# The recurrent half, retention's inputs, retention and the last projection of the second block's first layer as one stage, with heads in pairs and rotations by whole groups

## The reference, cut to what matters

```python
def hybrid_ab(h, w_in, conv_w, conv_b, ga_w, ga_b, gx_w, gx_b, lam, w_out):
    proj = h @ w_in
    y, xr, q, k, v, g = split(proj, six parts of 512 columns)
    xr = causal_depthwise_conv(xr, conv_w, conv_b)              # 4 taps
    lru_out = rg_lru(xr, ga_w, ga_b, gx_w, gx_b, lam) * gelu(y)
    ret_out = retention(q, k, v) * silu(g)                      # 8 heads of 64
    return concatenate([lru_out, ret_out], -1) @ w_out          # h = h + this

def rg_lru(x, ...):
    r, i = sigmoid(block_diag(x, ga_w) + ga_b), sigmoid(block_diag(x, gx_w) + gx_b)
    log_a = -8 * r * softplus(-lam)
    a, u = exp(log_a), sqrt(-expm1(2 * log_a)) * (i * x)
    return scan over tokens of  h = a * h + u

def retention(q, k, v):       # computed by the kernel over all 512 tokens at once
    q, k = rotary(q), rotary(k) / 8
    s = (q @ k.T) * decay     # decay[i, j] = g_head ** (i - j) for j <= i, else 0
    o = s @ v
    return (o - mean(o)) * rsqrt(var(o) + eps)                  # over each head's 64
```

## Time and profile before

| | us |
|---|---|
| median of 3 timed runs | 3396.03 |
| lowest and highest | 3384.46, 3397.12 |
| the profiled execution, its own time | 3386.9 |
| its span, first to last instruction | 3385.1 |
| TensorE busy | 2859.4 |
| VectorE busy | 1150.0 |
| ScalarE busy | 751.9 |
| POOL busy | 124.9 |

### The profile page before, as it was taken

One profiled execution on the slowest core, in us unless ns is written; L12 is line 12 of the kernel. 1 busy time (PEld: TensorE's weight loads), 2 busy tenths in 40 slices (PEclk: granted clock), 3 DMA queues, 4 the chain that ended last, 5 costly groups with the idle time before them and its releaser, 6 DMA issues.

```text
span 3385.1 us, 32012 instructions
## 1 busy us (share of the span) xinstructions
PE 2859.4 (84%) x13512; PEld 1848.2 (55%) x13512; DVE 1150.0 (34%) x1622; ACT 751.9 (22%) x1114; POOL 124.9 (4%) x116
## 2 busy tenths in 40 slices
PE   6877799888759879888845597899979999979997
PEld 4534453333348443323333473688869875558886
DVE  3434421111243431111145413332332368433233
ACT  2233300100122210100034110321221255232121
POOL 1200200000000200000010000000000000000000
PEclk8988889999979979999977798899987979989999
DMA  7852269999812069999911100223223200022230
GB/s 266 300 175 63 114 282 428 428 428 427 364 39 86 31 279 428 428 428 427 423 68 52 50 25 25 99 88 112 81 84 78 50 26 1 1 100 87 87 105 39
DMA packets 122255, 601.00 MB, mean 178 GB/s; under 512 B 7184, under 2 KB 12560, under 8 KB 96256
## 3 DMA queue, kind: packets, MB, share of 16 engines
q1 hardware_dynamic: 117056, 584.27, 43.7%
q0 software_dynamic: 5056, 14.69, 1.4%
HBM read 596.84 MB, written 2.10 MB: 177 GB/s over the span
## 4 chain that ended last, share of the span: by engine, by line
PE 65%; DMA 15%; DVE 12%; ACT 5%; issue 1%; POOL 0%; DVEq 0%; ACTq 0%; POOLq 0%
PE psum L281 63%; DVE scratch L231 5%; ACT scratch L269 5%; DMA weight_ring<-in_w_exp_down 5%; DMA weight_ring<-in_w_exp_up 4%; DMA scratch<-in_w_exp_down 3%; DMA weight_ring<-in_w_exp_gate 2%; PE psum L296 2%; DVE scratch L2906 1%; DVE scratch L244 1%; DVE scratch L264 1%; DVE scratch L237 1%; DVE scratch L1288 1%; DMA weight_ring<-in_w_mod 1%; ACT L269 0%
## 5 line engine op out<-in xcount | busy, mean ns | idle before, releaser
L281 PE MATMUL psum<-scratch,scratch 128*128 128x512 f32 (+13 forms) x9424 | 1943.0, 411 | 186.3 <-DVE scratch L231 110.0
L281 PEld LDWEIGHTS psum<-scratch,scratch 128*128 128x128 f32 (+4 forms) x9424 | 1418.9, 189 | 699.0 <-issue 338.9
L281 PE MATMUL psum<-weight_ring,scratch 128*64 128x512 f32 (+2 forms) x2752 | 710.5, 618 | 103.6 <-ACT scratch L269 36.0
L281 PEld LDWEIGHTS psum<-weight_ring,scratch 128*64 128x64 f32 (+2 forms) x2752 | 242.2, 146 | 526.8 <-issue 398.7
L231 DVE TENSOR_TENSOR scratch<-weight_ring,scratch 128x2048 fp32r<-128x2048 f32 (+2 forms) x110 | 241.9, 2199 | 596.6 <-ACT scratch L269 590.2
L269 ACT ACTIVATE scratch<-psum 128x512 f32<-128x512 f32 (+5 forms) x322 | 185.3, 575 | 889.3 <-PE psum L281 565.6
L269 ACT ACTIVATE scratch<-weight_ring 128x2048 fp32r<-128x2048 f32 (+2 forms) x110 | 202.9, 1844 | 660.7 <-PE psum L281 624.6
L296 PE MATMUL psum<-consts,scratch 128*128 128x128 f32 (+1 forms) x984 | 165.2, 315 | 181.4 <-DVE scratch L237 84.0
L296 PEld LDWEIGHTS psum<-consts,scratch 128*128 128x128 f32 (+1 forms) x984 | 129.7, 169 | 232.5 <-issue 95.7
L231 DVE TENSOR_TENSOR scratch<-scratch,psum 128x512 f32<-128x512 f32 x92 | 63.3, 688 | 563.0 <-PE psum L281 561.5
L231 DVE TENSOR_TENSOR scratch<-scratch,scratch 128x512 fp32r<-128x512 f32 (+10 forms) x346 | 211.9, 612 | 83.1 <-ACT scratch L269 72.5
(11 more groups left out here) (100 smaller groups left out, 619.2 us busy)
## 6 DMA issues: line engine op xcount, KB each, us to landing
weight_ring<-in_w_exp_gate SPq DMA_DIRECT2D x40, 2048.0 KB, 18.8
weight_ring<-in_w_exp_up SPq DMA_DIRECT2D x38, 2048.0 KB, 20.6
weight_ring<-in_w_exp_down SPq DMA_DIRECT2D x38, 2048.0 KB, 20.7
weight_ring<-in_ffn_w SPq DMA_DIRECT2D x28, 2048.0 KB, 7.8
scratch<-in_w_exp_up SPq DMA_DIRECT2D x26, 2048.0 KB, 20.6
scratch<-in_w_exp_down SPq DMA_DIRECT2D x26, 2048.0 KB, 18.1
weight_ring<-in_w_mod SPq DMA_DIRECT2D x24, 2048.0 KB, 8.8
scratch<-in_w_exp_gate SPq DMA_DIRECT2D x24, 2048.0 KB, 20.6
```

The source lines that it names most:

```text
L281: ins = T.eng.matmul(out, lhsT, rhs, start=start, stop=stop)
```

## The change

The stages `Recurrent`, `RetentionInputs`, `Retention` and `ResidualOut` become the one stage `Recurrent` (KEY `"ab_out"`); the fences between them are gone and every engine's order is written anew. The buffers are laid out so that the whole stage fits: `u` and later the rotated k, v, the gate and the scores share places of x and of the recurrence.

- POOL's small loads wait for the stage before the norm and no longer for the norm.
- The units come in the order x, y, q, k, v, g, two each. ScalarE and VectorE go through phases; phase n first splits unit n + 2 and then does what stands under it: convolution in 0 and 1, gelu in 2 and 3, sigmoids in 3 and 4, exp and tanh for all four groups in 4, roots in 5, scans in 6, rotations of q in 5 and of k in 7, the copies of the turned q, of v, of the turned k and the silu in 8 to 11.
- The gates on TensorE stand before and after the first q unit; the turns of q stand between the two v units, those of k between the two g units.
- The copies of the turned q into `qT` wait also until k is rotated, since the rotations' two temporaries lie in the places of `qT` and `kT`.
- One rotation is five VectorE operations over all four token tiles and all eight heads (one of 2048 elements a partition, four of 1024); k's factor is in the copy of the turned bank.
- Two heads of a pair are multiplied from the two halves of 64 partitions, without padding; decay, centring, squares and scaling run once for a pair, the product with the gate is on POOL.
- The last projection is in two halves: chunks 0 to 3 of `catT` (recurrence) are multiplied and added to `h` as fills between the pairs of heads, chunks 4 to 7 afterwards.

The diff, cut to its core (removed lines only where they show a difference):

```diff
 class Recurrent(Nothing):
-    KEY = "lru"
+    KEY = "ab_out"
+    LOW, HIGH = (0, 4), (4, 8)
+    FILL, O, TURNED = (0, 2), (2, 3), (3, 4)
...
     def sync(self, Y):
+        for u in self.units.values():
+            u.load(Y)
+        self.k.ring.load(Y, "decay", self.k.dram["decay"])
+        project_out_sync(self.k, Y, self.KEY, self.k.dram["ab_w_out_2"])
     def pool(self, G):
         self.norm.pool(G)
-        k.fence(G, self.norm.key)
+        k.fence(G, self.before)
         k.loads(G, "lru", [...])
+        k.loads(G, "ret", [(self.cos, d["ret_cos"]), (self.sin, d["ret_sin"])])
+        for p in range(4):
+            self.gated(G, p)
...
+    def unit_pe(self, T, name, i):
+        hi, lo = u.ready(T, i)
+        banks = k.psum.of(("ret", name)) if i else k.psum.take(T, ("ret", name), self.HIGH if name in "qv" else self.LOW, 4)
+        ...
+    def scores_pe(self, T, p, kt):
+        run = k.psum.take(T, ("ret s", p, kt), self.HIGH, 2)
+        ...
+        for i in range(2):
+            q = slice(64 * i, 64 * i + 64)
+            mm(T, run[:, i, 0:n], self.kT[q, p, kt * P:(kt + 1) * P], self.qT[q, p, kt * P:S], True, True, ...)
+    def values_pe(self, T, p):
+        T.wait_ge(*k.at("free", "ret s", p, NT - 1))
+        ...
     def pe(self, T):
         self.norm.pe(T)
         k.fence(T, self.norm.key)
+        for i in range(2):
+            self.features_pe(T, "x", i)
+        for i in range(2):
+            self.features_pe(T, "y", i)
+        for j in (0, 1):
+            self.gates_pe(T, j)
+        self.unit_pe(T, "q", 0)
+        for j in (2, 3):
+            self.gates_pe(T, j)
+        self.unit_pe(T, "q", 1)
+        for i in range(2):
+            self.unit_pe(T, "k", i)
+        self.unit_pe(T, "v", 0)
+        self.turned_pe(T, "q", self.rot_q, self.LOW)
+        self.unit_pe(T, "v", 1)
+        self.unit_pe(T, "g", 0)
+        self.turned_pe(T, "k", self.rot_k, self.HIGH)
+        self.unit_pe(T, "g", 1)
+        for p in range(4):
+            for kt in (0, 1):
+                self.scores_pe(T, p, kt)
+            if p:
+                self.values_pe(T, p - 1)
+            self.fill_pe(T, p if p == 0 else p + 1)
+            for kt in (2, 3):
+                self.scores_pe(T, p, kt)
+            if p == 0:
+                self.fill_pe(T, 1)
+            if p >= 2:
+                self.out_turn_pe(T, p - 2)
+        self.fill_pe(T, 5)
+        self.values_pe(T, 3)
+        self.fill_pe(T, 6)
+        self.out_turn_pe(T, 2)
+        self.fill_pe(T, 7)
+        self.out_turn_pe(T, 3)
+        ...
+        for t in range(NT):
+            for half in range(2):
+                self.project_pe(T, 1, t, half)
...
     def act(self, A):
+        for phase in range(-2, 12):
+            if phase + 2 < 12:
+                u, i = self.plan[phase + 2]
+                u.hi(A, i)
+            ...
+            if phase == 4:
+                A.wait_ge(*k.at("lru rate"))
+                for j in range(4):
+                    act(A, self.a[:, j, :], self.r[:, j, :], ACT.Exp, scale=self.small[3][:, j:j + 1])
+                for j in range(4):
+                    act(A, self.r[:, j, :], self.r[:, j, :], ACT.Tanh, ("lru tanh", j), scale=self.small[2][:, j:j + 1])
+            ...
+            if phase == 8:
+                self.turned_act(A, "q", self.qT, 1.0)
+        ...
+        for p in range(4):
+            A.wait_ge(*k.at("ret centred", p))
+            ...
+            act(A, self.sq[...], self.o[:, :, p * P:(p + 1) * P], ACT.Square, ("ret squared", p))
+            A.wait_ge(*k.at("ret mean square", p))
+            act(A, self.var[:, p, :], self.var[:, p, :], ACT.Sqrt, ("ret root", p))
+            if p >= 1:
+                self.out_act(A, p - 1)
...
     def dve(self, V):
-        fill(V, self.xr, 0.0)
-        V.wait_ge(*k.at("loaded", "lru"))
+        fill(V, self.xr[:, :, 0:4], 0.0, ("xr zero",))
+        ...
+        for p in range(4):
+            self.decayed(V, p, 0)
+            if p:
+                self.centred(V, p - 1)
+            self.decayed(V, p, 2)
+            if p == 0:
+                self.fill_dve(V, 0)
+                self.fill_dve(V, 1)
+            else:
+                self.fill_dve(V, p + 1)
+                self.scaled(V, p - 1)
+        self.fill_dve(V, 5)
+        self.centred(V, 3)
+        self.fill_dve(V, 6)
+        self.scaled(V, 3)
+        self.fill_dve(V, 7)
+        ...
+    def rotated(self, V, name, out):
+        ...
+        tt(V, a.rearrange("p (t h d) -> p t h d", t=NT, d=32), x.rearrange("p t (h d) -> p t h d", d=32),
+           cos.to_broadcast([P, NT, 16, 32]), ALU.mult)
+        ...
+        for i in range(2):
+            tt(V, bs[:, :, :, i, :], xs[:, :, :, 1 - i, :], sin, ALU.mult, *names)
+        for i, op in enumerate((ALU.subtract, ALU.add)):
+            tt(V, os[:, :, :, i, :], as_[:, :, :, i, :], bs[:, :, :, i, :], op, ...)
-class RetentionInputs(Nothing):
-    ...
-class Retention(Nothing):
-    ...
 def plan(k, out):
-    first = Recurrent(k, "scatter1")
-    inputs = RetentionInputs(k, first)
-    stages += [first, inputs, Retention(k, first, inputs), ResidualOut(k, "ab_out", Retention.KEY, d["ab_w_out_2"], first.catT)]
+    stages.append(Recurrent(k, "scatter1"))
```

More of the change, by code:

```diff
@@ new lines, in out_turn_pe, with project_pe @@
+    def out_turn_pe(self, T, p):
+        k = self.k
+        T.wait_ge(*k.at("ret gated", p))
+        bank = k.psum.take(T, ("ret turned", p), self.TURNED)
+        for t in range(NT):
+            tr(T, k, bank[:, t * P:(t + 1) * P], self.o[:, t, p * P:(p + 1) * P], *([("full", "ret turned", p)] if t == NT - 1 else []))
+    def project_pe(self, T, part, t, half):
+        k = self.k
+        T.wait_ge(*k.at("landed", (self.KEY, half)))
+        w = k.ring.pieces[(self.KEY, half)]
+        job = (self.KEY, part, t, half)
+        bank = k.psum.take(T, job, self.HIGH if part else self.FILL)
+        for c in range(4):
+            names = [("full", *job)] if c == 3 else []
+            if part and c == 3 and t == NT - 1:
+                names.append(("weights used", (self.KEY, half)))
+            mm(T, bank, self.catT[:, 4 * part + c, t * P:(t + 1) * P], w[:, 4 * part + c, :], c == 0, c == 3, *names)
@@ L2109, in pe @@
         k.fence(T, self.norm.key)
[L2110 to L2119, removed]
+        for i in range(2):
[35 more added lines that the diff above has]
+        for p in range(4):
+            T.wait_ge(*k.at("free", "ret turned", p))
+        for t in range(NT):
+            for half in range(2):
+                self.project_pe(T, 1, t, half)
         T.end(self.KEY)
@@ L2125, in act @@
         k.fence(A, self.norm.key)
[L2126 to L2148, removed]
@@ new lines, in dve @@
+        V.wait_ge(*k.at("landed", "decay"))
+        for p in range(4):
+            self.decayed(V, p, 0)
[12 more added lines that the diff above has]
+        self.scaled(V, 3)
@@ L2178, in dve @@
         ts(V, s1, rate, -1.0, None, ALU.mult, None, ("lru rate",))
[L2179 to L2186, removed]
-            tt(V, u, r, i, ALU.mult)
-            V.wait_ge(*V.last())
-            V.eng.tensor_tensor_scan(i, a, u, 0.0, ALU.mult, ALU.add).then_inc(*V.mark())
-            tt(V, self.catT[:, j, :], i, self.yT[:, j, :], ALU.mult, ("lru out", j))
@@ new lines, in decayed @@
+    def decayed(self, V, p, kt0):
+        k = self.k
+        decay = k.ring.pieces["decay"]
+        for kt in (kt0, kt0 + 1):
+            n = S - kt * P
+            at = sum(S - j * P for j in range(kt))
+            V.wait_ge(*k.at("full", "ret s", p, kt))
+            if p >= 3:
+                V.wait_ge(*k.at("full", "ret o", p - 3))
+            last = [("weights used", "decay")] if p == 3 and kt == NT - 1 else []
+            tt(V, self.sT[p % 3][:, :, at:at + n], k.psum.of(("ret s", p, kt))[:, :, 0:n], decay[:, 2 * p:2 * p + 2, 0:n], ALU.mult,
+               ("free", "ret s", p, kt), *last)
```

411 lines of the change are left out of this document (215 added, 196 removed).

## The result

The changed kernel takes 3256.46 us (median of 4 runs, 3252.21 to 3260.91), the kernel before 3393.15 (median of 4, 3384.46 to 3397.12). The ratio is 0.9601, with a 95% interval of 0.9577 to 0.9625. A second time, on another chip and with more runs of the kernel before, it was 0.9595 (0.9579 to 0.9610). The profiled execution took 3256.57 us, with a span of 3254.8 against 3385.1 before: 130.3 less.

What follows compares the result with a forecast made beforehand. The stage was taken as bound by a chain between engines, none full, leaving TensorE idle. TensorE's work plus remaining stalls summed to 250.6 us for 378.4, 128 less: 3259 profiled, 3263 stated, range 3244 to 3293.

Steps and rivals of the forecast that it cites:

- Start: From the norm's end to the first matmul: one hi, one lo and hand-overs left, 4.4 us in place of 9.85.
- x and y: The x and y projections: the same 192 matmuls in another order, 45.9 us.
- Recurrence, q, k, v, g: Gates' own work, 6.8 us for 49.5, chain hidden under projections; q, k, v, g with turns 100.3 for 141.8.
- The stall at q's turn: TensorE waits 3.6 us at q's transposes until VectorE's rotation has read k's banks.
- Retention with its eight fills: Scores, values, turns, stalls and clock dip 37.3 us in place of 75.5; the fills 3.45 each.
- The last forecast part: The last projection's matmuls not used as fills, with the last add; whole projection 55.2 + 0.7 us.
- The mode changes: Retention scores: tiling-mode changes drain TensorE; scores 9.9 us with the drain, 8.5 without any.
- 1, the clock low in retention: Retention part: clock stays low from short values matmuls and small gaps; +30 us, 3293; chance 0.07.
- 2, dearer rotations: Rotations of q and k: VectorE's PSUM operations cost up to double, delaying q's turn by 12 us; 3275; chance 0.12.
- 3, pairs that don't overlap: Retention scores: the two heads of a pair do not run side by side; +7 us, 3270; chance 0.05.
- 4, late weights: Weight loads: nine pieces each 14 us late would lose all the gain; 3390 and above beyond that; chance 0.01.
- 5, a wrong order in each phase: ScalarE and VectorE phases: waits in a wrong order, 12 phases x 5 us = 60; 3323; chance 0.04.

Runs made afterwards that it cites:

- two fence kernels: Changed kernel with POOL's small loads waiting for the norm again: 3252.86 us; the second with VectorE waiting for them before the first lo split too: 3263.20 us.
- lru_exposed: Changed kernel with all four gate groups ahead of q, and q waiting for the recurrences: 3281.32 us, ratio 0.9684 to the kernel before.
- rot_k_first: Changed kernel with VectorE rotating k after scans 0 and 1, before scans 2 and 3: 3251.85 us, ratio 0.9584 to the kernel before.
- both: Changed kernel, k rotated before the last two scans, pair 3 scaled before fill 6's add, last projection waiting per turned copy: 3247.96 us, ratio 0.9578.
- fills_last: Changed kernel with the eight fills and their adds behind the last turn, not between the pairs: 3273.91 us, ratio 0.9659 to the kernel before.
- fence_norm_wait: Changed kernel with small loads waiting for the norm and VectorE waiting for them before its first lo split: 3263.20 us, one run.
- scale_last: Changed kernel with scaling, gate and turns of all four pairs after the last values, behind fills 6 and 7: 3260.56 us, one run.
- rot_tiles: Changed kernel with rotations done tile by tile, seven operations of 256 elements each: 3265.78 us, ratio 0.9639 to the kernel before.

## Why the prediction was right, step by step

The forecast's sum was 250.6 us for the stage and 3259 against the profiled time; measured were 243.0 and 3256.6. The 2.4 us between the latter hide two errors of opposite sign: the stage came out 7.6 us shorter than summed, and what lies around it 5.1 longer. That the sum came this close is luck; the stage's own 7.6 is the size of the error. The stated 3263 had 4 us added for the kind of run, against a median of 3256.5.

**Start**: 4.4 forecast, 4.47 measured, with the reason shown by the two fence kernels. **x and y**: 45.9 against 45.2 (1750.12 to 1795.33).

**Recurrence, q, k, v, g**: 6.8 + 100.3 = 107.1 against 104.0. The gates and the five units ahead of q's turn take 62.2 where the forecast has 61.2; the gates are a part of it, 16 records in 3.65 us in `lru_exposed` where the forecast has 3.4. The stall at q's turn was forecast at 3.6 and is 3.79, with the right cause, as `rot_k_first` shows: VectorE's last read of k's banks, counted 111 us after the first x matmul, ended at 1861.22, 111.1 after it. What was mis-sized are the turns: I took 4.5 for q's and 3.5 for k's, and they take 2.52 and 1.72. The clock's price of 1.7 for the 96 matmuls behind q's turn is 1.1; the other 0.6 of the 1.7 found by `both` lie in the turn itself. The price "when warm" came from the 3.52 us for 16 transposes in the earlier trace rows. Asked for that window, the trace of the kernel before shows that TensorE was at its lower level there (0.54):

```profile
2061.77:2065.30 3.53, 3.52 (x16) 3.27 (x16) 0.69 (x1) 1.19 (x2) 0.00 (x0) 0.54 0.00 0
```

The row came straight after an idle time of 19.55 us. That window should have been read before it was called warm: 3.52 x 0.54 would have given 1.9, and 1.91 is what 16 transposes take in the changed kernel's line at a clock of 1.00.

**Retention with its eight fills**: 37.3 + 27.6 = 64.9 against 60.9. Again the turns are too dear (3.5 forecast, 2.2 measured), and the 2.3 us for a dip of the clock did not come: 1.00 in the whole stretch. Scores and values of a pair are 7.1 us in place of 7.5; the fills are 3.56 each in place of 3.45. The stalls, 0.57 + 0.64 + 0.69, are 1.9 in place of 1.8. The last forecast part, 28.3, is 28.5. All differences together: +0.1 - 0.7 - 3.1 - 4.0 + 0.2 = -7.5, the 7.6 but for rounding.

**The mode changes.** The Trainium skill (TensorEngine Tiling, "Key Properties") says that a change of the tiling mode drains TensorE. The trace shows no cost of it that could be told for certain. A pair's scores are 2.7 us, 1.81 for the first half (6.38 less the 4.57 of 40 values records) and 0.86 for the second; side by side at the ideal of the forecast it would be 2.13. The 0.5 us above that are the most that the drains can cost here, 2.2 us over four pairs; no run separates them from anything else.

**What I had not counted.** The rest of the span got 3.1 us longer (1263.1 to 1266.2 from the stage's last add), and the norm ended 2.0 later (1743.63 to 1745.64); the forecast had both unchanged. 135.4 - 2.0 - 3.1 = 130.3, the difference of the spans. The norm's end lies between 1741.9 and 1750.8 in the variants' traces, without any tie to the edit. For the 3.1 see the last section.

**The rivals.** 1, the clock low in retention: not so with fills (1.00), but fills_last shows that it does come without them (0.70 at the end). 2, dearer rotations: the plain price holds, 4.81 us. 3, pairs that don't overlap: refuted, and its price of 7 is 8.3 behind k's turn. 4, late weights: no wait in the stage is on a DMA. 5, a wrong order in each phase: there is one such place, k's rotation behind four scans, and it costs 5.7 us, not 60.

**Where the 135.4 us came from.** By undoing one part at a time: the recurrence under q and k 26.8, the fills 16.9, the rotations by groups 10.8, the pairs side by side 9.4, the first split ahead of the wait 6.8 (`fence_norm_wait`). Less what lies ahead of the edit these are 25.4, 15.9, 10.8, 8.3 and 6.8, together 67.2. The earlier rates and the hand-over from the recurrence to q's splits add 13.1, seen in `lru_exposed`. The remaining 55.1 us were not undone by themselves. In the trace of before, waits of 59.6 us bear on them. At the eight turns of q and k, each of which waited for one tile's rotation, they are 7.5, 3.2, 3.1 and 3.1 us for q's, 7.9 and three times 5.0 for k's, 40.0 together, with the clock low behind them; at the norm of the heads they are 19.55 us in one wait. The first waits of q's and of k's turns there:

```profile
1880.49 1.12 PE L296 MATMUL psum<-consts,scratch 128*128 128x128 f32 x4 [7.48 <-DVE scratch L264]
...
1925.78 1.12 PE L296 MATMUL psum<-consts,scratch 128*128 128x128 f32 x4 [7.94 <-DVE scratch L237]
```

Both kinds of work now lie under another unit's or pair's matmuls. That this is the rest was argued from the two traces, not shown by a run; for the norm of the heads `scale_last` shows a part, 9.0 us when its scaling stands at the end. The single effects need not add up, since one stall may hide another.

## What to carry to other kernels

Where a stage is a chain between engines and none is full, lay independent matmuls under each chain, price the stage as TensorE's own work plus what each joint still waits, and count to each joint with VectorE's and ScalarE's own queues: the stall came within 0.2 us. Take a price for a short operation only from a window whose granted clock has been read, since after an idle time of 19.55 us it was near twice the real one here. Work laid into the gaps of this loop paid twice, for the gaps and for the clock that fell without it.

## What was not expected of the hardware

**The clock behind one and the same wait.** The feed-forward part at the end has not been touched. In both kernels TensorE waits 2.2 us ahead of its second and of its third group of projections. The first rows: the kernel before. The second: the changed kernel at the same instructions, with the columns of the earlier trace rows.

```profile
3000.60:3010.60 10.00, 10.00 (x38) 8.13 (x39) 2.28 (x1) 0.00 (x0) 0.00 (x0) 0.85 0.00 0
...
3311.70:3320.00 8.30, 8.29 (x37) 6.87 (x37) 2.29 (x1) 1.24 (x1) 0.00 (x0) 1.00 0.18 65
```

```profile
2867.59:2877.59 10.00, 10.00 (x33) 8.05 (x34) 2.27 (x1) 0.00 (x0) 0.00 (x0) 0.74 0.00 0
...
3179.73:3188.03 8.30, 8.30 (x29) 6.69 (x30) 2.29 (x1) 1.23 (x1) 0.00 (x0) 0.79 0.20 65
```

Behind the last wait the clock is 1.00 before and 0.79 after: the last 240 matmul records take 54.70 and 56.33 us. In the first 10 us of the part it is 0.85 and 0.74, and the 576 records that begin there take 132.28 and 133.28. The 768 between them take 174.4 in both. That is 2.6 of the 3.1 us; the rest lies ahead of this part. Both kernels did the same again in a second execution, to 0.1 us. Most variants are 2 to 3 us longer behind the stage than the kernel before, but `scale_last` is only 0.5 longer, and in `rot_tiles` the last group is as fast as before:

```profile
3196.20 54.69 PE L281 MATMUL psum<-scratch,scratch 128*128 128x512 f32 x240 [2.23 <-DVE scratch L231]
```

So one and the same wait costs its own 2.2 us or 1.6 more. It is the same for one kernel each time and differs between kernels that are alike in this part, as at the start of the stage, where the clock was 0.84 or 0.69 behind the same start. What decides it was not settled: no run shifted the part by a chosen time.

**Short work at either level.** 16 transposes of 128x128 in one row take 1.91 us at a clock of 1.00, and 3.52 at 0.54.

**Operands of VectorE.** Four PSUM banks in one instruction with a broadcast operand, and in two of the three swapped halves as well, cost next to nothing above the plain price: 4.81 us for one of 128x2048 and two of 128x1024, against 2.29 + 2 x 1.23.
